# Panels of the expert up matrices issued by ScalarE, gate and down panels by SyncE

## What is computed

```
hidden_e = silu(x_e @ w_gate[e]) * (x_e @ w_up[e])     # w_gate, w_up: 1024 x 1024
y_e      = hidden_e @ w_down[e]                        # w_down:       1024 x 1024
tokens  += spread_back(gate_weight_e * y_e)
```

## Time and profile before

| | us |
|---|---|
| median of 3 runs | 2728.86 |
| lowest, highest | 2728.52, 2733.14 |
| the profiled execution | 2730.3 |
| its span in the trace | 2728.3 |
| PE busy | 2356.9 (86%) |
| DVE busy | 583.0 (21%) |
| ACT busy | 373.3 (14%) |
| DMA, mean over the span | 239 GB/s |

### The profile page before, as it was taken

One profiled execution on the slowest core, in us unless ns is written; L12 is line 12 of the kernel. 1 busy time (PEld: TensorE's weight loads), 2 busy tenths in 40 slices (PEclk: granted clock), 3 DMA queues, 4 the chain that ended last, 5 costly groups with the idle time before them and its releaser, 6 DMA issues.

```text
span 2728.3 us, 39444 instructions
## 1 busy us (share of the span) xinstructions
PE 2356.9 (86%) x17780; PEld 1541.6 (57%) x17780; DVE 583.0 (21%) x1235; ACT 373.3 (14%) x851; POOL 30.9 (1%) x56
## 2 busy tenths in 40 slices
PE   8999999989999999899989897888799876656564
PEld 6788688477886884445545554554454543323222
DVE  1201100023011000534443121222311441101112
ACT  1211000012210000215433000000102320000000
POOL 0000000000000000000000000000000000000000
PEclk9999999999999999999989999999999988888878
DMA  8444675353436774300042999999920068999997
GB/s 297 151 137 145 235 269 209 130 210 133 151 123 232 262 249 139 133 0 1 1 185 95 426 425 427 426 426 426 386 81 0 0 247 357 427 428 426 428 427 303
DMA packets 165387, 651.93 MB, mean 239 GB/s; under 512 B 8039, under 2 KB 55523, under 8 KB 140515
## 3 DMA queue, kind: packets, MB, share of 16 engines
q1 hardware_dynamic: 161392, 639.66, 60.0%
q0 software_dynamic: 3312, 8.79, 1.0%
q10 hardware_dynamic: 514, 0.94, 0.1%
HBM read 648.27 MB, written 1.08 MB: 238 GB/s over the span
## 4 chain that ended last, share of the span: by engine, by line
PE 54%; issue 28%; DMA 13%; DVE 3%; ACT 1%; DVEq 0%; ACTq 0%; POOL 0%; POOLq 0%
PE psum L1962 11%; DMA ring<-in_moe_w_up 10%; PE psum L1817 8%; PE psum L1894 6%; PE psum L1977 5%; PE psum L438 4%; PE psum L1882 3%; PE psum L631 3%; PE psum L562 2%; PE psum L430 2%; DMA ring<-in_moe_w_gate 2%; PE psum L1944 1%; PE psum L1795 1%; PE psum L1843 1%; DMA ring<-in_moe_w_down 1%
## 5 line engine op out<-in xcount | busy, mean ns | idle before, releaser
L631 PE MATMUL psum<-ring,arena 128*32 128x256 f32 x6144 | 402.2, 417 | 177.1 <-DMA ring<-in_moe_w_up 94.9
L631 PEld LDWEIGHTS psum<-ring,arena 128*32 128x32 f32 x6144 | 216.7, 118 | 359.6 <-issue 153.5
L1962 PE MATMUL psum<-ht,ring 128*128 128x256 f32 x1408 | 310.8, 382 | 2.1 <-ACT ht L2017 2.1
L1962 PEld LDWEIGHTS psum<-ht,ring 128*128 128x128 f32 x1408 | 266.9, 191 | 41.8 <-issue 5.7
L648 PE MATMUL psum<-ring,lnp 128*32 128x256 f32 x3072 | 195.6, 409 | 77.3 <-DMA ring<-in_moe_w_down 73.7
L648 PEld LDWEIGHTS psum<-ring,lnp 128*32 128x32 f32 x3072 | 106.5, 116 | 165.2 <-issue 56.0
L438 PE MATMUL psum<-ring,ht 128*128 128x512 f32 x448 | 194.9, 594 | 0.0
L1894 PE MATMUL psum<-ht,ring 128*128 128x256 f32 x768 | 166.7, 379 | 0.0
L1894 PEld LDWEIGHTS psum<-ht,ring 128*128 128x128 f32 x768 | 145.9, 190 | 20.7 <-issue 1.0
L1977 PE MATMUL psum<-ring,arena 128*128 128x512 f32 x352 | 151.5, 593 | 2.3 <-DVE arena L2237 2.3
L1387 DVE TENSOR_TENSOR arena<-psum,arena 32x512 f32<-32x512 f32 (+1 forms) x128 | 70.8, 553 | 386.0 <-PE psum L648 384.7
(11 more groups left out here) (336 smaller groups left out, 1934.3 us busy)
## 6 DMA issues: line engine op xcount, KB each, us to landing
ring<-in_moe_w_gate SPq DMA_DIRECT2D x64, 2048.0 KB
ring<-in_moe_w_up SPq DMA_DIRECT2D x64, 2048.0 KB
ring<-in_moe_w_down SPq DMA_DIRECT2D x64, 2048.0 KB
ring<-in_w_in SPq DMA_DIRECT2D x52, 1024.0 KB
ring<-in_ada_w SPq DMA_DIRECT2D x48, 1024.0 KB
ring<-in_w_ffn_gate SPq DMA_DIRECT2D x22, 1024.0 KB
ring<-in_w_ffn_up SPq DMA_DIRECT2D x22, 1024.0 KB
ring<-in_w_ffn_down SPq DMA_DIRECT2D x20, 1024.0 KB
```

The costliest lines, as they stand in the source:

```text
L631: last = mm(bank[32 * j:32 * j + 32, SPLIT * m:SPLIT * m + SPLIT], x_four[:, k, e % 4, SLOTS * m:SLOTS * m + SLOTS], slot[:, k % 4, SPLIT ...
L1962: last = mm(bank[:, SEQ * u:SEQ * u + SEQ], slot[:, k, SEQ * u + P * h:SEQ * u + P * h + P], xT[:, k, :], start=k == 0, stop=k == KT - 1)
```

## The change

The body of the inner loop becomes a function `matrix(eng, layer, i)`, which issues the two panels of the i-th matrix of a layer from the engine that it is given, with the same waits for the ring slot. `sync` calls it for the first three matrices and from then on for g and y alone. `scalar` calls it for u: as it comes to matrix number `at` in its own walk, and matrix `at + 2` is a u, it issues that one before it does its own work for the step. The slots, the bytes, the waits for the slots and all arithmetic stay.

```diff
+def matrices():
+    return [(kind, e) for kind, e in expert_steps() if kind in "guy"]
...
+    def matrix(eng, layer, i):
+        kind, e = matrices()[i]
+        name = {"g": "gate", "u": "up", "y": "down"}[kind]
+        rows = I[f"moe_w_{name}_2"][layer][e].rearrange("(p j) n -> p j n", p=P)
+        at = banks.stage_panels[f"exp{layer}"][0] + 2 * i
+        for h in range(2):
+            first, _, _ = banks.release[at + h - RING]
+            eng.wait_ge(pe_done, first)
+            slot = (at + h) % RING
+            eng.dma_start(view(ring[:, slot, :], PANEL // D, D), rows[:, 4 * h:4 * h + 4, :]
+                          ).then_inc(panel_in[slot], 32)
...
         def experts(layer):
-            w = {k: I[f"moe_w_{m}_2"][layer] for k, m in (("g", "gate"), ("u", "up"), ("y", "down"))}
-            for kind, e in expert_steps():
-                if kind not in w:
-                    continue
...
+            for i, (kind, e) in enumerate(matrices()):
+                if i < 3 or kind != "u":
+                    matrix(sp, layer, i)
+                n[0] += 2
...
+            order, at = matrices(), 0
             for kind, e in expert_steps():
+                if kind in "guy":
+                    if at >= 1 and at + 2 < len(order) and order[at + 2][0] == "u":
+                        matrix(act, layer, at + 2)
+                    at += 1
                 if kind == "g":
                     bank, freed = full_bank(act, stage, ("g", e))
```

## The result

| | before | after |
|---|---|---|
| median of 10 runs, us | 2728.95 | 2736.63 |
| lowest, highest | 2727.51, 2733.14 | 2733.15, 2739.77 |
| span of the profiled execution | 2728.3 | 2735.0 |

The ratio of the times is 1.0021, with a 95% interval of 1.0012 to 1.0031: the changed kernel is slower by about 6 us, 3 to 8 by the interval. The medians are 7.7 us apart. Two later series gave 1.0021 and 1.0022.

A forecast was written before the change was run, and what follows sets the result against it. Both expert layers were taken as bound by the DMA engines' rate. Layer 0's tail +6.5, layer 1 and issues 0, on the profiled 2730.3 give 2736.8; the median, 1.4 lower, is 2735.4 us, 0.24% slower, range 2727 to 2747.

The forecast's parts named there:

- What bounds it: Both expert layers run at the rate of the DMA engines, share 1.00 and 0.99; TensorE has time to spare.
- Issue cost and Silu: ScalarE's 60 up-panel issues, 22 us, lie where it waits and hold up no Silu: 0.
- Sharing one to one: SP's and ScalarE's queues advance together at equal rates; u lands early, g and y ahead of it late.
- The order at the end: At a layer's end y14b lands two panels before the end, where before it landed four before.
- The sign of the rate: In the profile after, GB/s in the expert stretches stay unchanged within 1%.
- The tail of layer 0: After y14b lands at 1937.9, TensorE's remaining work is exposed and ends at 1957.9 instead of 1951.4: +6.5 us.
- The second bound, +8.2: Upper bound for layer 0's end, +8.2 us, if the wait before y14b also lowers the clock.
- Layer 1, 0 between -1.2 and +2.4: End of layer 1: 1.2 us earlier, or +2.4 with two more panels at the low clock; taken as 0.
- Rival 2: DMA engines run dry at step x (u4, u8, u12): 2741 with 4 us of delay, 2747 with 6; chance 0.15.
- the 2.0 us of cover: At step x, SP's queue holds 19.7 us of work while u4 flows at t + 17.7, leaving 2.0 us.
- Rival 1: Queues served in order of issue, or ScalarE's at less than its half: nothing changes, 2729 us; chance 0.20.
- rival 3: Second queue fills holes between uneven landings, 15 us in layer 0; with half of that 2720 us; chance 0.08.

The follow-up runs named there:

- both faults mended: Changed kernel with u15 of layer 0 on SyncE again and u4, u8, u12 issued ahead of ScalarE's part of step x: 2727.52 and 2728.29 us, ratio 0.9994.

## Why the prediction was right, point by point

- **What bounds it**: right. Layer 1, where TensorE has about half the work for the same bytes, lost nothing. Half the matmuls in layer 0 gave some 3 us, in one execution.
- **Issue cost and Silu: 0.** Right. ScalarE is as busy as before (373.0 us over the span), and layer 1 with all its issues is not slower.
- **Sharing one to one**: right, 116 packets against 115.
- **The order at the end**: right. y14b is the last panel that TensorE waits for, and y14b, u15, y15 follow in one run. Moving u15 alone back takes away the loss, and moving it alone makes 4 us of it.
- **The sign of the rate, "unchanged within 1%"**: missed by a little in layer 0, with 420 GB/s for 425 (422 and 423 in the other two profiles of the changed kernel). It isn't the loss: the kernel with u15 back moved 421 and lost nothing, the one with u15 alone moved kept 424 and lost 4 us.
- **The tail of layer 0, +6.5**: the mechanism and the sum hold (measured +5.8 in the first pair of profiles, 7 us between the ratios of the changed kernel and the one with u15 back), but two terms were off, with opposite signs. The last landing was read as 1947.8, on the ground that the row of 8.80 us ended with a panel of 3.66 on which TensorE had waited. It had not: the row runs without a stop, and the clock was at half in the middle of that row, by three windows of 1 us in the kernel before:

```profile
1944.00:1945.00 1.00, 1.00 (x16) 0.69 (x12) 0.00 (x0) 0.00 (x0) 0.00 (x0) 0.50 0.77 231
1945.00:1946.00 1.00, 1.00 (x16) 0.64 (x12) 0.00 (x0) 0.00 (x0) 0.00 (x0) 0.50 0.91 313
1946.00:1947.00 1.00, 1.00 (x13) 0.58 (x9) 0.00 (x0) 0.00 (x0) 0.00 (x0) 0.50 0.99 362
```

  In the kernel with layer 1 alone changed, whose layer 0 is that of before, the last panel started at 1946.32 after 0.63 us of waiting for its DMA, 455.9 us after the layer's first product; in the time of the earlier trace rows that is 1945.9. This landing is an estimate, from another execution; of the one of the earlier trace rows it is known only that TensorE did not wait for it. What is measured is y14b: it began 445.9 us into the layer, not 447.8 (444.7 and 446.9 in the other profiles), so it was put 1.9 us too late. The other term is y14b itself: I took 3.66 for it, "since the rows of layer 0 show 1.00 of the clock". After a wait of 4.52 us it took 5.35. The second bound, +8.2, had that in it.
- **Layer 1, 0 between -1.2 and +2.4**: -1.7, a little beyond the bound. y14b began 439.8 us into the layer, exactly where two panels before the old last landing put it (2698.5 - 2258.7). After y14b's 3.45 all panels ran at the fast clock, y15's two in 3.66, and TensorE no longer sat before the last panel.
- **Rival 2, gaps at x, taken as 0**: this was partly real. Transfer for 5.9 us is missing in the first profile, and about 2 us may be time (see above for what is open). Of the steps of the 2.0 us of cover, ScalarE's held. y2b was let go at 1579.78 and u4 issued at 1595.85, 16.1 us later, as worked out (16.2): the low clock made y2b 1.7 longer, and in return the issue went out 3.9 us after x began, not 5.4. The step that failed is SyncE's: 19.7 us of work in its queue from that moment. The GB/s fall from 1594 on, after 14 us. So some of y3 and g4 must have been moved when TensorE was let go on y2b. How much of that is the time from a panel's last byte to its waiter, and how much are engines that run ahead of the slowest, stays open.

```profile
1579.78 5.35 PE L658 MATMUL psum<-ring,lnp 128*32 128x256 f32 x64 [4.54 <-DMA ring<-in_moe_w_down]
1584.94 7.09 PE L641 MATMUL psum<-ring,arena 128*32 128x256 f32 x128
1591.96 7.41 PE L607 MATMUL psum<-ht,arena 128*128 128x128 f32 x64
```

```profile
1595.85 0.35 ACTq L361 DMA_DIRECT2D ring<-in_moe_w_up  x1
```

- **Rival 1 and rival 3** are out. Whatever makes rival 3's landings uneven, the second queue did not fill the holes: with both faults mended layer 0 moved 424 GB/s, not more than before. The rival's time, 2720, also takes off 7.5 us twice, where half of its 15 us in layer 0 is 7.5 once. With one it is 2727.9, inside the stated range and not below it.

The sum came out close (2735.4 against 2736.63) partly because its errors cancelled, which was luck: y14b 1.9 too late, its clock 1.7 too little. Layer 1 was 1.7 too much with nothing against it: in the first pair of profiles the two layers together give +4.1, and 2.6 of the 6.7 us between the two spans lie outside them, in stretches where one execution differs from the next. Against the other profile of the old layer 0 they give +5.9. What the gaps at x cost is no further term: they come before y14b and are contained in its 445.9. Single profiles differ by some 2 us, so that no finer account can be given.

## What to carry to other kernels

Where a stream of weights filled the DMA engines, a second queue gave no rate here (420 to 424 GB/s for 425). It changed the order in which transfers land, and the transfers that had to share the rate were those that the consumer wanted first. Judge such a move at the end of the stream: take each of the last panels, add to its landing the consumer's whole work from there on, and keep the largest sum. With the up matrices it was enough to keep the last one in the order in which it is wanted, and the other 58 panels cost nothing that the ratio shows. With the gate matrices the last three matrices kept their order and 5 us were lost all the same, so the sum has to be made for the panels before them too. And an engine that issues DMAs between its other steps had better issue ahead of any step that itself waits for the consumer; here this was worth 0 to 3 us.

## What the runs showed of the hardware that was not expected

- The dips of the mean DMA rate vary from one execution to the next: at the steps x and elsewhere in layer 0 transfer worth 6.7, 4.3 and 4.0 us was missing in three profiles of the same kernel, while the layer took 467.1, 467.1 and 468.2 us. So the length of the layer did not follow the missing transfer one to one. That some engines run ahead of the slowest, so that a dip of the mean leaves the slowest at work, would fit with this and with the windows in which the share falls by steps (0.65, 0.70; 0.50, 0.38) and not to zero. It was not tested.
- The spacing of a weight stream went with the number of matmuls beside it: with 42 packets of instructions in 391 us of layer 0 the panels were 4.99 us apart, with half the matmuls and 21 packets 4.95. That the packets are the cause isn't shown.
- In layer 0's window few long waits went with a lower granted clock than many short ones. With 52 waits in 397 us, nearly all of 0.9 to 1.4 us and four of 2.6 to 2.9, it was 1.00; with 16 waits, ten of them of 3.9 to 6.2 us, it was 0.93. The idle time was not more but less, 59 us for 68.
